# A two-group hybrid trunk layer: entry statistics, modulation sums and first border's weights in another order

## What is computed

```python
mod = silu(c) @ w_mod + b_mod          # 9 x 1024 values for each of the two groups
h = rms_norm(x, n_pre[0]) * (1 + sc0) + sh0
x = x + 0.5 * g0 * rms_norm(swiglu(h, f_in[0], f_out[0]), n_post[0])
h = rms_norm(x, n_pre[1]) * (1 + sc1) + sh1
y, st = token_mixer(h, ...)            # mLSTM and attention, one input projection
x = x + g1 * rms_norm(y, n_post[1])
h = rms_norm(x, n_pre[2]) * (1 + sc2) + sh2
x = x + 0.5 * g2 * rms_norm(swiglu(h, f_in[1], f_out[1]), n_post[2])
```

## Time and profile before

| what | value |
|---|---|
| median of three executions | 1704.51 us (1703.63 to 1705.38) |
| the profiled execution's own time | 1704.33 us |
| its span | 1702.6 us |
| mean granted clock of TensorE | 0.997 of full speed |
| TensorE busy | 1679.4 us, 99% |
| DVE busy | 1044.2 us, 61% |
| ACT busy | 745.3 us, 44% |
| transfers | 189.66 MB, mean 111 GB/s |

### The profile page before, as it was taken

The page is one execution under the profiler, slowest core; times in us unless marked ns, Lnnn a source line. Parts: engine busy times, 40 slices in busy tenths (PEclk is TensorE's granted clock), DMA queues, the critical chain, the costliest instruction groups (busy, mean ns, idle before and its releaser), DMA issues.

```text
span 1702.6 us, 27823 instructions
## 1 busy us (share of the span) xinstructions
PE 1679.4 (99%) x11327; PEld 1545.3 (91%) x11327; DVE 1044.2 (61%) x1779; ACT 745.3 (44%) x1402; POOL 0.2 (0%) x4
## 2 busy tenths in 40 slices
PE   8999999999999999999999999999999999999998
PEld 6998899989889888999999888889889989998997
DVE  5777687548666224555537877775646834872775
ACT  6312255325574332443445554553564433551452
POOL 0000000000000000000000000000000000000000
PEclk9999999999999999999999999999999999999999
DMA  9787222322613215233243211111621221332233
GB/s 386 279 319 262 75 66 84 100 61 89 210 54 111 84 62 113 82 95 87 81 149 118 67 52 42 42 41 58 228 87 50 75 87 62 100 97 77 74 105 144
DMA packets 56790, 189.66 MB, mean 111 GB/s; under 512 B 7464, under 2 KB 16472, under 8 KB 53848
## 3 DMA queue, kind: packets, MB, share of 16 engines
q1 hardware_dynamic: 56664, 187.89, 33.1%
HBM read 170.67 MB, written 16.54 MB: 110 GB/s over the span
## 4 chain that ended last, share of the span: by engine, by line
PE 89%; DVE 4%; ACT 3%; issue 1%; DMA 0%; DVEq 0%; ACTq 0%
PE psum L762 9%; PE psum L764 9%; PE psum L763 9%; PE psum L744 7%; PE psum L745 7%; PE psum L746 7%; PE psum L872 4%; PE psum L873 4%; PE psum L874 4%; PE psum L1288 2%; PE psum L1270 2%; PE psum L834 2%; PE psum L836 2%; PE psum L835 2%; PE psum L1248 2%; PE psum L1173 1%
## 5 line engine op out<-in xcount | busy, mean ns | idle before, releaser
L1906 DVE TENSOR_TENSOR wlo<-raw,whi 128x1024 fp32r<-128x1024 f32 x120 | 146.8, 1224 | 310.4 <-ACT whi L1382 310.3
L1382 ACT CAST whi<-raw 128x1024 fp32r<-128x1024 f32 x120 | 125.5, 1046 | 257.2 <-PE psum L874 125.1
L762 PE MATMUL psum<-g_hi,whi 128*128 128x320 f32 x656 | 209.4, 319 | 0.2 <-ACT gate L1724 0.2
L764 PE MATMUL psum<-g_hi,wlo 128*128 128x320 f32 x656 | 202.7, 309 | 0.0
L763 PE MATMUL psum<-g_lo,whi 128*128 128x320 f32 x656 | 202.6, 309 | 0.0
L762 PEld LDWEIGHTS psum<-g_hi,whi 128*128 128x128 f32 x656 | 123.2, 188 | 4.9 <-issue 1.9
L872 PE MATMUL psum<-whi,g_hi 128*128 128x512 f32 x320 | 125.0, 390 | 0.0
L874 PE MATMUL psum<-whi,g_lo 128*128 128x512 f32 x320 | 124.5, 389 | 0.0
L873 PE MATMUL psum<-wlo,g_hi 128*128 128x512 f32 x320 | 124.5, 389 | 0.0
L763 PEld LDWEIGHTS psum<-g_lo,whi 128*128 128x128 f32 x656 | 123.3, 188 | 0.7
L764 PEld LDWEIGHTS psum<-g_hi,wlo 128*128 128x128 f32 x656 | 123.1, 188 | 0.0
(11 more groups left out here) (446 smaller groups left out, 4386.2 us busy)
## 6 DMA issues: line engine op xcount, KB each, us to landing
raw<-in_w_ffn_in SPq DMA_DIRECT2D x88, 512.0 KB, 3.6
raw<-in_w_mix SPq DMA_DIRECT2D x77, 512.0 KB, 4.1
raw<-in_w_ffn_out SPq DMA_DIRECT2D x44, 512.0 KB, 3.6
direct<-in_w_mod SPq DMA_DIRECT2D x7, 2048.0 KB, 9.4
mw<-in_w_mod SPq DMA_DIRECT2D x14, 768.0 KB, 5.4
mw<-in_w_mod SPq DMA_DIRECT2D x8, 1024.0 KB, 16.8
gate<-gate_keep SPq DMA_DIRECT2D x24, 320.0 KB, 5.2
gate_keep<-gate SPq DMA_DIRECT2D x20, 320.0 KB, 4.6
```

The source lines that it names most:

```text
L762: mm(out, wh[:, k, :], hi[:, k, cols], start=(k == 0), stop=False)
L764: last = mm(out, wl[:, k, :], hi[:, k, cols], start=False, stop=(k == nk - 1))
L1382: copy((to or whi[t.slot])[:, :, :], raw[t.raw][:, :, :]).then_inc(w_hi, 1)
L1906: tt(lo[:, :, :], raw[t.raw][:, :, :], hi[:, :, :].bitcast(F32), ALU.subtract).then_inc(raw_free, 1)
```

## The change

It has three parts. (1) Entry: each square gets its own place in `x_sq`, which lies where h will be; DVE adds the squares in pairs, four additions in place of seven; TensorE sums the four pairs by accumulating in PSUM, eight matmuls in place of two; the eight `keep_busy` matmuls between are dropped; tile 0's split moves behind the root, on ACT and on DVE. (2) The sums of the first phase stand at seven places in place of eleven, and the direct loads are issued behind other tiles. (3) First border: tiles 3 and 4 are split at the end of the last `seven`; the mixer's first tiles 0 and 1 are split in row 0, 2 in row 1, 3 in row 2; row 0 takes its last two steps in another order; and the first two rows of tokens are loaded behind all weight tiles of the FFN instead of behind the third from last.

```diff
-SUM_AFTER = {3: 0, 6: 1, 9: 2, 11: 3, 14: 4, 16: 5, 18: 6}
-DIRECT_AFTER = {5: 0, 6: 1, 8: 2, 10: 3, 12: 4, 14: 5, 16: 6}
-DIRECT_LOAD = {12: 2, 13: 3, 15: 4, 17: 5, 19: 6}
+SUM_AFTER = {3: 0, 6: 1, 8: 2, 12: 3, 14: 4, 16: 5, 18: 6}
+DIRECT_AFTER = {6: (0, 1), 8: (2,), 12: (3, 4), 14: (5,), 16: (6,)}
+DIRECT_LOAD = {13: (2, 3), 15: (4,), 18: (5, 6)}
...
     pairs = [[(f, j + o) for f in range(2) for o in range(2)] for j in range(0, nj - 2, 2)]
+    if l == 0 and c == 0:
+        return [s for p in pairs for s in p] + [(f, nj - 2 + o) for f in range(2) for o in range(2)]
...
+        x_sq = at("x_sq", [P, KC, N], F32, h_at)
...
                     load_tile(c)
-                    if c in DIRECT_LOAD:
-                        load_direct(DIRECT_LOAD[c])
+                    for m in DIRECT_LOAD.get(c, ()):
+                        load_direct(m)
...
-                    if c == T_MIX - 3:
-                        sp.wait_ge(prod_done, KEEP + 5 * (FIRST_PAIRS[2] - 1) + 4)
-                        load_tokens(slice(0, 2))
+                sp.wait_ge(prod_done, KEEP + 5 * (FIRST_PAIRS[2] - 1) + 4)
+                load_tokens(slice(0, 2))
                 load_tokens(slice(2, NT))
...
             def first_stats():
-                pe.wait_ge(sq_sum, KC - 1)
-                for h in range(2):
-                    last = mm(half_out(2, h), ones_d, rb[:, HCOLS[h]], start=True, stop=True)
+                for j in range(KC // 2):
+                    pe.wait_ge(sq_sum, j + 1)
+                    for h in range(2):
+                        last = mm(half_out(2, h), ones_d, x_sq[:, 2 * j, HCOLS[h]],
+                                  start=(j == 0), stop=(j == KC // 2 - 1))
                 last.then_inc(ystat_mm, 1)
...
             pe.wait_ge(silc_ready, 2)
-            for m in range(3, KC - 1):
-                pe.wait_ge(sq_sum, m)
-                keep_busy(psum[:, 0, 0:2 * P], BUSY_SUM)
             first_stats()
...
ACT, seven(), last pair:
                         split(Tile(base + 2 * n + 4), row_weights(2 * net(base), 2, base + 2 * n + 2)[0], 0)
+                        for u in range(3, 5):
+                            split(t.plus(u), row_weights(2 * net(base), u, t.c)[0], ut.n + 3)
...
ACT, border():
-                for u in range((3, 5, 3)[l], ROW_TILES[l]):
+                for u in range(5, ROW_TILES[l]):
...
-                if l == 0:
-                    first_split(0, ended)
-                    first_split(1, ended)
...
                     root_y(l, c, base)
-                    if c == 0:
-                        if l < 2:
-                            first_split((2, 0)[l], ended)
-                        if l < 2:
-                            first_split((3, 1)[l], ended)
+                    if c == 0 and l < 2:
+                        first_split(0, ended)
+                        first_split(1, ended)
+                    elif l == 0 and c < 3:
+                        first_split(c + 1, ended)
...
ACT, first_normed() and the entry:
                 take_rows(0)
+                split(Tile(0))
...
-                reuse(0, k)
-                fn(sq[k % 2][:, :], x[:, k, :], ACT.Square).then_inc(ysq_in, 1)
-            split(Tile(0))
+                fn(x_sq[:, k, :], x[:, k, :], ACT.Square).then_inc(ysq_in, 1)
...
DVE, seven(), last pair:
                     pair_product(n, s)
-                    if not rows_next:
+                    if rows_next:
+                        for u in range(3, 5):
+                            split(Tile(base + 2 * n + 2 + u), row_weights(2 * net(base), u, base + 2 * n + 2))
+                    else:
                         split(Tile(base + 2 * n + 3))
                     pair_low(n, s)
...
DVE, first_normed() and the entry:
                 first_mod(0)
+                split(Tile(0))
                 times_root(1)
...
+            def add_squares(j):
+                dve.wait_ge(ysq_in, 2 * j + 2)
+                one, two = x_sq[:, 2 * j, :], x_sq[:, 2 * j + 1, :]
+                tt(one, one, two, ALU.add).then_inc(sq_sum, 1)
...
DVE, border():
                     if l < 2 and c == 0:
-                        first_split((2, 0)[l])
-                        first_split((3, 1)[l])
+                        first_split(0)
+                        first_split(1)
                     elif l < 2 and not (l == 0 and c == NT - 1):
+                        if l == 0 and c < 3:
+                            first_split(c + 1)
                         next_low(c - 1)
```

More of the change, by code:

```diff
@@ L47 @@
 LAGS = (0, 1, 3)
-BUSY_FIRST, BUSY_SUM, BUSY_TURN = 12, 2, 3
+BUSY_FIRST, BUSY_TURN = 12, 3
 MOD_LATER = NMOD * KC // MOD_T - MOD_FIRST
@@ L934, in sums_after @@
                     sum_mod(SUM_AFTER[c])
-                if c in DIRECT_AFTER:
-                    sum_direct(DIRECT_AFTER[c])
+                for m in DIRECT_AFTER.get(c, ()):
+                    sum_direct(m)
             def turn_mod_rows():
@@ L1462, in inv_root @@
                 fn(rb[:, :], rb[:, :], ACT.Exp, scale=-0.5).then_inc(rb_ready, 1)
-            def reuse(l, m):
-                if m >= 2:
-                    act.wait_ge(sq_sum, (KC - 2) * l + max(m - 2, 1))
             def root(l, c, src, slot, count, out, half=None):
@@ L2156, in first_split @@
                     split(Tile(nxt + u), first_weights(l, u, nxt))
-                for u in range((3, 5, 3)[l], ROW_TILES[l]):
+                for u in range(5, ROW_TILES[l]):
                     split(Tile(base + u), row_weights(l, u, base))
-                if l == 0:
-                    first_split(0)
-                    first_split(1)
                 for c in range(NT if l < 2 else NT - 1):
@@ L2258, in _ @@
                               ALU.add).then_inc(cols_in, 1)
-            for m in range(KC):
-                add_square(0, m)
-            split(Tile(0))
+            for j in range(KC // 2):
+                add_squares(j)
             root_ready(0)
```

## The result

The changed kernel takes 1711.97 us in the median of five executions (1710.33 to 1714.89), the kernel before beside it 1704.51: a ratio of 1.0048, 95% interval [1.0036, 1.0059], or 8.2 us slower (0.48%). The profiled execution took 1710.33 us with a span of 1708.6, so +6.0 against the profiled one of before; a stretch in which one profile differs from another by 1.6 us and more, with the same code, is shown at the end.

The account below looks back on a forecast made before the run. TensorE, busy for 99% of the span, was taken as the bound. Terms -0.7 - 0.8 + 3.9 + 1.8 + 2.15 = +6.35 on 1704.33 gave 1710.7 us, with an 8-in-10 range of 1704.0 to 1713.5.

Parts of the forecast that it names:

- Entry, -0.7: At the entry: statistics start earlier, but the fourth w_mod0 block's landing limits the gain to 0.7 us; bounds 0 and 1.9.
- The landing of w_mod0 at 24.9: Entry: the fourth w_mod0 block lands at 24.9, against use at 25.62, so the fourth modulate step can't start earlier.
- Fewer places, -0.8: First phase: sums at 7 places instead of 11, each place less saving 0.2 us, together 0.8; bounds 0.5 and 1.3.
- Late block 2, +3.9: After tile 8: TensorE wants direct block 2 at 103.9, it lands at 107.8, a 3.9 us stall; bounds 3.6 and 5.0.
- The landing of 8.5 us: Block 2's direct load, issued at 99.26 with nothing queued before it, lands 8.5 us later; 9.4 in a loaded queue.
- Clock behind it, +1.8: Behind the stall after tile 8: TensorE's clock falls as at the border, costing 1.8 us; bounds 0 and 3.5.
- Border, +2.15: First border: late post rows hold row 0's scale, +0.15 us; extra splits in rows 1 and 2, +2.0; bounds -0.1 and +3.
- rival 2: First border: post rows don't hold row 0; landing at 462 gains 3.9 us, total +0.3, 1704.6 us; chance 0.15.
- Rival 1: After tile 8: block 2 is there in time, only 0.4 us for DVE remains; total +1.05, 1705.4 us; chance 0.08.
- rival 3: After the stall behind tile 8: TensorE's clock holds; total +4.55, 1708.9 us; chance 0.14.
- rival 4: Entry: statistics don't come forward, so it gives 0; 1711.4 us; chance 0.57 together with the forecast.
- rival 5: Stall and border: more lost at both, interleaved blocks, clock low for 6 us; total +10.5, 1714.8 us; chance 0.06.

Follow-up runs that it names:

- run 3: Changed kernel with ten unread matmuls on TensorE ahead of the wait for block 2 after tile 8: 1710.17 us, ratio 1.0037 to the kernel before.
- run 8: Changed kernel with early direct loads, x_tok's first rows loaded as before, post rows issued first and 6 keep-busy matmuls at the head: 1700.02 us, ratio 0.9975.
- run 9: Changed kernel with direct loads behind the earlier tiles and the border's part undone, leaving entry and places alone: 1703.46 us, ratio 0.9995 to the kernel before.
- run 1: Changed kernel with direct loads behind tiles 12, 13, 15, 17 and 19 again: 1703.40 us, ratio 1.0002 to the kernel before.
- run 7: Changed kernel with 6 in place of 12 unread keep-busy matmuls at its start: 1711.32 us from one execution, ratio not timed.
- run 6: Changed kernel with x_tok's first two rows loaded as before and post rows issued ahead of other tokens and mixer tiles: 1707.82 us, ratio 1.0021.
- run 10: run 8 with all four of the mixer's first splits in row 0: 1703.38 us, ratio 0.9995 to the kernel before.
- run 2: Changed kernel with block 3's direct load behind tile 14, apart from block 2's: 1712.16 us, ratio 1.0055 to the kernel before.
- run 4: Changed kernel with the border's part undone, entry and sums as changed: 1712.31 us, ratio 1.0050 to the kernel before.
- run 5: Changed kernel with only x_tok's first two rows loaded as before, behind the third tile from last: 1710.62 us, ratio 1.0035.

## Why the prediction was right or wrong, step by step

The forecast was +6.35 us; +7.5 between the medians and +8.2 by the ratio were measured. The main mechanism, a late block 2 with a lower clock behind it, and the sign held. That the sum came so near is partly luck: in the trace, stall and clock came out 2.4 us dearer than forecast, counting 0.4 for sum 2 beside them, places and border came out 1.4 cheaper, and 1.6 more fell away behind the border, in a stretch that no part of the change touches. The terms:

- **Entry, -0.7.** It gave 0.5 in this trace, and for another reason than the step had; the near hit is luck. "The twelve added records lie beside squares that are still to come" failed: the keep-busy matmuls run until 4.2 us after the first pair sum was begun (7.25), so all sixteen records ran behind them. The landing of w_mod0 at 24.9, which I had as the limit, was none in the changed kernel's own trace; it became one in runs 3, 8 and 9, where statistics ended earlier, and the fourth step then started at 26.21, 24.53 and 25.92. It moves by more than the gain that was at stake: in the eight traces with the entry as changed the fourth step starts between 25.03 and 26.21, in the mean at 25.50, only 0.1 under the one trace of the kernel before. What the entry gives is open.
- **Fewer places, -0.8.** From run 1: -1.4 ahead of the border, less the entry (25.03 against 25.62: -0.6) and the 0.42 for sum 2, leaves -1.2. The term was 0.4 short, inside its bound of 1.3.
- **Late block 2, +3.9.** The place, the cause and the wait were right; the size was 5.07. The landing of 8.5 us was mis-sized: it took 10.3, beyond the 9.4 that I held for the worst. That upper bound came from two of the seven direct loads, though the lower one looked at all seven, and the trace of before has them all. Its view of line 513, and the load issued at 61.23:

```profile
L513 SPq DMA_DIRECT2D direct<-in_w_mod x7: 328/432/433, 41.9 to 149.2; - x7
...
DMA to landing us min/median/max: 8.5/9.4/11.2
...
direct<-in_w_mod SPq DMA_DIRECT2D x1, 2048.0 KB, 10.1
```

Five of them landed in 8.5 to 9.5 us, the first two in 11.2 and 10.1. With 11.2 as the worst case the bound of the stall would have been 6.6 and not 5.0, and every stall measured in this slot (3.91 to 5.78) lies under it; run 7's 3.91 is the forecast's own 3.9. The other direct issues of the changed kernel land after 8.3 to 11.5 (the last is the median of two). The estimate by the Trainium skill (DMA: Bandwidth & Descriptors, Anatomy of one DMA), 7.6 us from the block's issue, is further off. The page fits its formula to transfers issued by GpSimd, and these are issued by SyncE; no run here tests that difference.
- **Clock behind it, +1.8.** 2.6 by the trace (what 6.37 leaves when -0.5, -1.2, +0.4 and +5.07 are taken off), 1.9 to 2.4 by run 3, 1.4 to 2.8 over all traces with the stall. Inside the bounds.
- **Border, +2.15.** +1.3 in the changed kernel's trace, 2.0 in run 1's. The post rows do hold row 0, as the forecast and not rival 2 had it: scale(0) came 0.6 earlier than before, against the shift, where I had 0.15 later. The extra splits cost 0.94 each, 1.9 in place of 2.0. What I did not price was what it gave away: with row 0 ready 5 us earlier, the chain was held by loads whose order is free, and run 6 takes 4.6 us from that.

Rival 1 (block there in time) and rival 3 (clock holds) are excluded by the rows above; rival 4's observation (no gain from earlier statistics) was half true; rival 5 had the stall (5 us) and the 6 us of lower clock nearly right, but priced that clock at 3.5 and the border at 3.0; the median stayed under its 1714.8. Two sums of the rivals are off without weight for the forecast: the estimate of 7.6 gives a stall of 3.0, not 3.1, and post rows landed at 462 would gain 5.6 less the 2.0 of the splits, 3.6 and not 3.9.

## What to carry to other kernels

Before a load is moved one slot later, compare the slot plus the worst landing of all loads of that kind in the old trace (11.2 here, not the 8.5 of the nearest one) with the moment the data is wanted; a stall of 5 us on a full TensorE cost 7.8 here. When an engine's row gets ready earlier, look at once at what it waits for next and whether that load stands behind others that nobody wants yet. And when work is cut into more, earlier matmuls, check that nothing fills the queue in front of them.

## What the runs showed of the hardware

- In the changed kernel the clock fell some 3.5 us into the stall, before any work came, and stayed at 0.50 for nearly 7 us, to 114. Behind the waits of 2.11 us in run 9 and 2.13 in run 3 it fell too, 0.8 us after TensorE had begun to work again. Behind one of 1.23 us in run 8 it did not, and a wait filled with 20 records kept 1.00. A long wait is not the only way there: in the entry of runs 7 and 10, with no wait over 0.91 us, the clock had a mean of 0.57 and 0.58 from 18 to 22 us.
- Issuing two post-row loads took SyncE 6.63 us behind a loaded queue (changed kernel) and 1.01 us ahead of it (run 6). SyncE's next issue came only behind them, at 466.71 in the changed kernel.
- Between the mkt and cp copies, code that no kernel here changes, the shift against before moved by -1.6 (changed kernel, run 1), 0 (runs 2, 3, 6 to 10) or +1.6 to +1.5 us (runs 4 and 5). Busy time by stretch there, the kernel before first, then the changed one (the clock is the third column from the end):

```profile
590.00:595.00 5.00, 5.00 (x45) 4.48 (x45) 1.74 (x3) 1.05 (x1) 0.00 (x0) 0.82 0.35 96
595.00:600.00 5.00, 5.00 (x20) 4.04 (x19) 0.00 (x0) 1.76 (x3) 0.00 (x0) 0.84 0.03 12
```

```profile
590.00:595.00 5.00, 5.00 (x24) 4.14 (x23) 2.71 (x2) 1.05 (x1) 0.00 (x0) 1.00 0.10 39
595.00:600.00 5.00, 5.00 (x48) 4.30 (x47) 1.23 (x1) 1.05 (x1) 0.00 (x0) 1.00 0.18 70
```

A short dip of the clock there comes and goes from trace to trace, and the shift follows it: the two traces at -1.6 have none (1.00 from 585 to 610 us), those at 0 have one as long as that of the kernel before, and in runs 4 and 5 it is twice as long (0.50 from 600 to 605, and 0.85 to 0.97 on both sides). An effect of 1 us can't be read from one profile's total. Whether this is also why the profiled execution of the changed kernel lies 1.6 us under its median is not shown; run 1's has no dip either and lies at its median.
